# Weight slabs split into high and low parts in halves, in a ring of four half slabs instead of two whole ones

## The chip, the cores and the metric

The kernel runs on one core of a Trainium2 chip. The metric is the device time of one launch in microseconds (us), as the median of several runs. Five engines work side by side and meet only at semaphores: TensorE (PE) does the matrix products, VectorE (DVE) and ScalarE (ACT) the elementwise work, GpSimd (POOL) some more of it, and SyncE (SP) issues the DMAs. Each engine works through its own instructions in the order in which they are written.

## The reference, cut to what matters

Two transformer-like blocks in float32 on a sequence of 512 tokens of width 1024: a convolution block, a squared-ReLU feed-forward layer with a gated per-layer embedding, forgetting attention with a second such layer; then a block with three branches (RG-LRU, block attention, attention to a memory of 256 tokens) and a gated feed-forward layer with a short convolution. Nearly all of the arithmetic is products of activations with weight matrices.

```python
hn = rmsnorm(h, mix_norm[i]);  h = h + conformer_conv(hn, ...)      # layer 0: pw1, 31-tap conv, layernorm, silu, pw2
k, v, c = shared_kv(h, kv_norm, w_kvf, b_f)                         # layer 1
h = h + fox_attention(hn, w_q, w_o, k, v, c)
h = h + square(relu(rmsnorm(h, ffn_norm[i]) @ ffn_w1[i])) @ ffn_w2[i]
h = h + sigmoid(rmsnorm(h, ple_norm[i]) @ w_gate[i]) * (p[i] @ w_proj[i])
# second block
proj = rms_norm(x, mix_norm_gain) @ w_in                            # xa, ga, qm, km, vm, qx, gates
y_a = rg_lru(causal_dwconv(xa, ...)) * gelu(ga); y_b = moba_attention(qm, km, vm); y_c = cross_attention(qx, mem)
x = x + sum_n(gate_n * (y_n @ w_branch[n])) @ w_out
x = x + (gelu(causal_dwconv(h @ w_ffn_gate, ...)) * (h @ w_ffn_up)) @ w_ffn_down
```

## The kernel before, in words

All activations stay in SBUF as (128 partitions = channels, 512 tokens), eight such chunks for a width of 1024. Each float32 product is made of three matmuls on rounded parts: `w_hi*x_hi + w_hi*x_lo + w_lo*x_hi` (`three`, L489 to L492). A rounded part `w_hi` is a copy of the weights by ACT, and `w_lo = w - w_hi` is a subtraction by POOL.

Weights come in 176 slabs of 128x2048 floats. A slab holds two columns of output blocks (8 chunks of 128 rows each), so PE makes two blocks of 24 matmuls from it, each in one of four PSUM banks (`gp`). A slab goes through four hands:

- SP loads it into one of two places of `raw` (`slab`, L281), once POOL has made `w_lo` of the slab two before it (its semaphore `w_lo_done`).
- ACT copies it to `w_hi` (`next_w`, L778 to L786). This is called at chosen places of ACT's program for the slab after the one named, and waits until PE has finished the slab that had the place before (`blk_done`). `w_hi` and `w_lo` have two places each.
- POOL makes `w_lo` (`slab`, L363 to L366), in the order of the slabs, between its other work.
- PE uses it (`slab_ws`, L494; `slab_xs`, L511, where the weights are the moving operand) after `w_lo_done`.

The order is written out by hand for each engine; loops (`Fori`) repeat a body. The places of interest:

- The first convolution (`tap_products` on ACT, L828; `add_taps` on POOL, L414; `conv` on DVE): channels are worked in four pairs of chunks. For a pair DVE multiplies and adds 22 taps, while ACT makes 9 products that POOL adds into `pool_sum` (16 additions for a pair). Within this, the blocks of the next pair are fetched from PSUM (`pair_out`, `T<-gp,rstd`), ACT makes the sigmoids (L826), and slabs of the pair after that are split: at `t == MID_TAP` and at `t == GATE_TAP` on ACT, after `t == 5` and at the end on POOL. Once, in the first pair, DVE also scales the memory (`mem_raw`, eight instructions).
- The start of a feed-forward layer (`ffn_layer`, L931): PE starts on the new slabs while DVE and ACT make `rstd` (`finish_norm`, L803). PSUM banks come free only when `rstd` is there.
- The gates after a feed-forward layer (L958 to L975): for each block DVE does six to seven operations on SBUF tensors and ACT four.
- The RG-LRU (L1087 to L1100, L1595 to L1620): four steps, each a chain of PE, ACT (`lru_hi`, sigmoids, tanh, sqrt) and DVE (seven linked operations `link_l`), beside the blocks of `gqm` and `gkm`.
- The branches (`branch`): DVE multiplies a block with its gate and adds it to `merged`.
- SP waits for POOL's memsets of `wga` and `wgx` (L448, L449) before it loads them, and issues the next slab after them.

## Time and profile before

| | |
|---|---|
| median of 3 runs | 2306.7 us (2306.33 to 2308.54) |
| span of the profiled execution | 2308.7 us (first to last instruction; the page gives no other time of this execution) |
| PE busy | 2153.5 us, 93% |
| DVE, POOL, ACT busy | 1154.3, 939.4, 791.1 us |
| granted TensorE clock, mean | 0.971 of full speed |
| DMA | 196.74 MB, mean 85 GB/s |

The page and the views list instructions by the line of the kernel, the engine, the operation and the tiles (`out<-in`). The busy share alone doesn't say what an engine's work costs: what PE waits for, and when, is in the view of waits and in PE's timeline, where a figure in brackets is the idle time just before an instruction, with what ended it. The line of a helper (L490 to L492, L1146, L1149) stands for all its callers, so the tiles tell which stage a row is of.

### The profile page before, as it was taken

Reading aid. Unit: us, or ns where it says so; the run is one execution under the profiler, and the core shown is the slowest. Engines: PE = TensorE matmul, PEld = TensorE weight load, DVE = VectorE, ACT = ScalarE, POOL = GpSimd, SP = SyncE. Lnnn points to the kernel's source line nnn. Section 1 sums busy time; section 2 is a strip of 40 time slices with the busy share of each in tenths; the row PEclk is TensorE's granted clock in tenths of the full one; section 3 lists DMA queues with packets and bytes.
Section 4 is the critical chain, followed back from the end, with each engine's and each line's share of the span. In section 5 each row is a group of like instructions: output and inputs, shape, how many; then the busy total and the mean of one; then the engine's idle time right before and its main releaser. Section 6 shows DMA issues by size and latency. Waiting matters only on the chain.

```text
span 2308.7 us, 27336 instructions
## 1 busy us (share of the span) xinstructions
PE 2153.5 (93%) x10068; PEld 1764.5 (76%) x10068; DVE 1154.3 (50%) x1624; ACT 791.1 (34%) x1044; POOL 939.4 (41%) x306
## 2 busy tenths in 40 slices
PE   7547999999999999999999998999899999999997
PEld 6445788888878987778888876777777878888885
DVE  5996543233473545462342557328444357445364
ACT  5445422122442146321221344324225243222232
POOL 4785344344343420334444342343253334434332
PEclk9878999999999999999999999999999999999998
DMA  4121222322322211222222321132220222322231
GB/s 178 37 73 55 91 91 93 108 91 91 106 77 93 101 46 36 100 73 98 103 91 93 107 89 58 55 114 73 73 92 1 92 91 91 109 92 91 92 108 55
DMA packets 30717, 196.74 MB, mean 85 GB/s; under 512 B 4384, under 2 KB 4512, under 8 KB 7984
## 3 DMA queue, kind: packets, MB, share of 16 engines
q1 hardware_dynamic: 30640, 195.68, 24.4%
q8 instruction: 52, 0.85, 0.2%
q14 instruction: 25, 0.20, 0.0%
HBM read 193.54 MB, written 2.13 MB: 85 GB/s over the span
## 4 chain that ended last, share of the span: by engine, by line
issue 43%; PE 38%; POOL 13%; DVE 5%; ACT 1%; POOLq 0%; ACTq 0%; DVEq 0%
PE gp L490 11%; PE gp L492 11%; PE gp L491 11%; POOL w_lo L366 11%; PE ms L692 2%; PE gp L644 2%; POOL pool_sum L422 2%; PE ms L629 1%; DVE T L1602 1%; DVE T L1146 1%; DVE U L1601 1%; DVE xc L1149 0%; DVE U L1146 0%; DVE U L1447 0%; DVE merged L1146 0%
## 5 line engine op out<-in xcount | busy, mean ns | idle before, releaser
L366 POOL TENSOR_TENSOR w_lo<-raw,w_hi 128x2048 fp32r<-128x2048 f32 x176 | 813.3, 4621 | 1192.9 <-ACT w_hi L786 1187.4
L490 PE MATMUL gp<-a_hi,w_hi 128*128 128x512 f32 x1440 | 572.4, 397 | 56.9 <-DVE T L1146 27.2
L491 PE MATMUL gp<-a_lo,w_hi 128*128 128x512 f32 x1440 | 566.0, 393 | 0.0
L492 PE MATMUL gp<-a_hi,w_lo 128*128 128x512 f32 x1440 | 565.9, 393 | 0.0
L490 PE MATMUL gp<-b_hi,w_hi 128*128 128x512 f32 (+1 forms) x1216 | 476.0, 391 | 41.3 <-POOL b_lo L434 27.4
L786 ACT ACTIVATE w_hi<-raw 128x2048 fp32r<-128x2048 f32 x175 | 333.5, 1906 | 436.0 <-PE gp L492 431.2
L491 PE MATMUL gp<-b_lo,w_hi 128*128 128x512 f32 (+1 forms) x1216 | 472.6, 389 | 0.0
L492 PE MATMUL gp<-b_hi,w_lo 128*128 128x512 f32 (+1 forms) x1216 | 472.4, 389 | 0.0
L490 PEld LDWEIGHTS gp<-a_hi,w_hi 128*128 128x128 f32 x1440 | 274.2, 190 | 121.8 <-DVE T L1146 28.0
L491 PEld LDWEIGHTS gp<-a_lo,w_hi 128*128 128x128 f32 x1440 | 274.2, 190 | 58.6 <-issue 2.0
L492 PEld LDWEIGHTS gp<-a_hi,w_lo 128*128 128x128 f32 x1440 | 273.7, 190 | 57.8
L490 PEld LDWEIGHTS gp<-b_hi,w_hi 128*128 128x128 f32 x1216 | 230.2, 189 | 94.7 <-POOL b_lo L434 27.8
L1146 DVE TENSOR_TENSOR h<-gp,h 128x512 f32<-128x512 f32 x104 | 71.9, 692 | 411.8 <-PE gp L492 411.8
L492 PEld LDWEIGHTS gp<-b_hi,w_lo 128*128 128x128 f32 x1216 | 230.4, 189 | 46.9
L491 PEld LDWEIGHTS gp<-b_lo,w_hi 128*128 128x128 f32 x1216 | 230.6, 190 | 46.6 <-issue 0.7
L1146 DVE TENSOR_TENSOR T<-gp,rstd 128x512 f32<-128x512 f32 x144 | 98.5, 689 | 301.4 <-PE gp L492 297.7
L1149 DVE SCALAR_TENSOR_TENSOR ms<-u_pad,par,ms 128x512 f32<-128x512 f32 x168 | 111.7, 747 | 0.0
L795 ACT ACTIVATE sqb<-h 128x512 f32<-128x512 f32 x63 | 39.8, 632 | 183.6 <-DVE h L1146 156.3
L1149 DVE SCALAR_TENSOR_TENSOR U<-T 128x512 f32<-128x512 f32 x64 | 100.2, 1566 | 2.2
L422 POOL TENSOR_TENSOR pool_sum<-pool_sum,sqb 128x512 f32<-128x512 f32 x64 | 81.5, 1308 | 26.9 <-ACT sqb L841 26.9
L1042 ACT ACTIVATE T<-T,nmax 128x128 f32<-128x128 f32 (+1 forms) x96 | 53.8, 561 | 64.3 <-DVE U L1447 41.8
L1124 ACT ACTIVATE T<-T,par 128x512 f32<-128x512 f32 x24 | 17.4, 724 | 158.0 <-DVE T L1149 158.0
(255 smaller groups left out, 2100.4 us busy)
## 6 DMA issues: line engine op xcount, KB each, us to landing
raw<-w_hbm SPq DMA_DIRECT2D x176, 1024.0 KB, 4.9
fbias<-negc_scratch SPq DMA_DIRECT2D x16, 256.0 KB, 3.1
h<-x_hbm SPq DMA_DIRECT2D x4, 512.0 KB, 7.1
out_hbm<-h SPq DMA_DIRECT2D x4, 512.0 KB, 2.7
mem_raw<-mem_hbm SPq DMA_DIRECT2D x1, 1024.0 KB, 12.1
p_raw<-p_hbm SPq DMA_DIRECT2D x2, 512.0 KB, 9.1
par<-par_hbm SPq DMA_DIRECT2D x1, 264.5 KB, 5.2
wga<-w_a_hbm SPq DMA_DIRECT2D x2, 64.0 KB, 2.3
```

Of the source, the lines that this page charges most:

```text
L366: g.tensor_tensor(w_lo[:, s], raw[:, s], f32(w_hi[:, s]), ALU.subtract).then_inc(w_lo_done, 1)
L422: g.tensor_tensor(pool_sum[:, s], pool_sum[:, s], sqb[:, s], ALU.add).then_inc(pool_conv, 1)
L490: pe.matmul(o, wh, xh, start=start, stop=False)
L491: pe.matmul(o, wh, xl, start=False, stop=False)
L492: return pe.matmul(o, wl, xh, start=False, stop=stop)
L644: m = pe.matmul(gp[:, s % 2, 0:vw], probT[s % 2][:, kb * P:kb * P + P], v_of(j, s % per, kb), start=(kb == 0), stop=(kb == n_of[s % per] - 1))
L692: pe.matmul(ms[:, s % 2, 0:w], qs[:, hh, qb * P:qb * P + P], k, start=True, stop=False)
L786: act.activation(w_hi[:, s], raw[:, s], ACT.Copy).then_inc(w_hi_done, 1)
L795: act.activation(dst, h[:, c], ACT.Square).then_inc(sq_done, 1)
L1042: return act.activation(prob[:, s % 4, 0:w], prob[:, s % 4, 0:w], ACT.Exp, scale=-1.0, bias=nmax[:, s % 4:s % 4 + 1], accum_out=rsum[:, s ...
L1146: return v.tensor_tensor(o, a, b, op)
L1149: return v.scalar_tensor_tensor(o, a, s, b, op0, op1)
```

## The change

Each slab is still loaded as a whole into `raw`, in two places. But `w_hi` and `w_lo` are now rings of four places of half a slab (128x1024), and a half is one block of 24 matmuls (for `slab_xs`, where all 8 chunks of rows are needed, PE waits for both halves). A half takes every second run of 128 columns of the slab's eight rows (`part`; two runs of 512 of two rows, or of 256 of four, and for `slab_xs` the first or second 1024 elements). ACT's `next_w` copies the half three places ahead (`AHEAD`), once the block before the named one is done. PE's matmuls and their order are the same; the memory's mean comes after the first block of the second slab as before. The calls of `next_w`, and the order of POOL's work, are rewritten.

```diff
+PART = SLAB // 2
+RING = 4
+AHEAD = RING - 1
-        w_hi, w_lo = sb("w_hi", [P, 2, SLAB], F32R), sb("w_lo", [P, 2, SLAB], F32R)
+        w_hi, w_lo = sb("w_hi", [P, RING, PART], F32R), sb("w_lo", [P, RING, PART], F32R)
+        def part(pos, d=0):
+            r = rows_of[pos.const + d]
+            i = pos.slot(4, d)
+            q, n = i % 2, SLAB // r // 2 if r else PART
+            src = raw[:, i // 2].rearrange("p (k c) -> p k c", k=r or 2)
+            src = src[:, q:q + 1] if not r else src[:, :, q * n:q * n + n]
+            return src, lambda ring: ring[:, pos.slot(RING, d)].rearrange("p (k c) -> p k c", k=r or 1)
...
@@ SyncE @@
-                    q.wait_ge(w_lo_done, pos.at(-1))
+                    q.wait_ge(w_lo_done, Pos(2 * pos.const, 2 * pos.step, pos.i).at(-2))
-            slabs(wo["slab"] + 2, gxg["slab"])
+            slabs(wo["slab"] // 2 + 3, br[2]["slab"] // 2 + 3)
             for t, name in ((wga, "w_a"), (wgx, "w_x")):
@@ GpSimd @@
+                src, at = part(pos)
-                g.tensor_tensor(w_lo[:, s], raw[:, s], f32(w_hi[:, s]), ALU.subtract).then_inc(w_lo_done, 1)
+                g.tensor_tensor(at(w_lo), src, f32(at(w_hi)), ALU.subtract).then_inc(w_lo_done, 1)
...
-                    if t == MID_TAP + 2:
-                        slab(Pos(4, 2, i))
+                    if t == MID_TAP + 2 and not extra:
+                        for s in range(2):
+                            slab(Pos(memkv["slab"] + 4 + s))
                 if extra:
-                    slab(Pos(5, 2, i))
+                    for s in range(RING):
+                        slab(Pos(8 + s, RING, i))
...
-            slabs(wo["slab"] + 1, gxg["slab"])
+            slabs(wo["slab"] + AHEAD, br[2]["slab"] + AHEAD)
             g.wait_ge(lo_done, xat["split"] + 4)
             g.memset(wga[:], 0.0).then_inc(wg_zero, 1)
@@ TensorE @@
-                s = sp_.slot(2)
-                cc = 16 // kk
+                s = sp_.slot(RING)
+                cc = 8 // kk
                 pe.wait_ge(w_lo_done, sp_.at(1))
@@ ScalarE @@
             def next_w(sp_, bp):
-                s = sp_.slot(2, 1)
-                act.wait_ge(raw_ready[s], 16 * (sp_.turns(2, 1) + 1))
+                src, at = part(sp_, AHEAD)
+                s = sp_.slot(RING, AHEAD)
+                act.wait_ge(raw_ready[s // 2], 16 * (sp_.turns(RING, AHEAD) + 1))
                 if bp.const > 0:
                     act.wait_ge(blk_done, bp.at())
-                act.activation(w_hi[:, s], raw[:, s], ACT.Copy).then_inc(w_hi_done, 1)
+                act.activation(at(w_hi), src, ACT.Copy).then_inc(w_hi_done, 1)
...
                 pw1_gates(Pos(4, 4, i), lambda n, s, o: colp(i)(n, s, o + 2))
-                next_w(Pos(4, 2, i), Pos(8, 4, i))
+                for s in range(RING):
+                    next_w(Pos(5 + s, 4, i), Pos(5 + s, 4, i))
-            next_w(Pos(1), Pos(2))
+            for s in range(1, 5):
+                next_w(Pos(s), Pos(s))
             pw1_gates(Pos(0), colp(0))
-            next_w(Pos(2), Pos(4))
...
-                    if s == 0:
-                        next_w(sp_, bp)
+                    if k == 0:
                         finish_norm(pw2 if l == 0 else wo)
+                    up_hi(f, Pos(f["slab"] + k), Pos(f["blk"] + k), Pos(fu), H_, k)
...
             for j, (at, s) in enumerate(((gqm, 0), (gqm, 1), (gkm, 0), (gkm, 1))):
-                next_of(at, s)
+                next_of(at, 2 * s)
                 act.activation(T[:, 3], T[:, 2], ACT.Sqrt).then_inc(l_act, 1)
+                next_of(at, 2 * s + 1)
```

How the instructions move at three places. First, GpSimd in the first pair of the first convolution (`pool_sum` are the tap additions), before:

```order
L366 TENSOR_TENSOR w_lo<-raw,w_hi 128x2048
L373 REGISTER_ALU
L373 COMPARE_AND_BRANCH
L422 TENSOR_TENSOR pool_sum<-pool_sum,sqb 128x512 x10
L366 TENSOR_TENSOR w_lo<-raw,w_hi 128x2048
L422 TENSOR_TENSOR pool_sum<-pool_sum,sqb 128x512 x6
L366 TENSOR_TENSOR w_lo<-raw,w_hi 128x2048
```

and in the changed kernel:

```order
L383 TENSOR_TENSOR w_lo<-raw,w_hi 128x1024
L392 REGISTER_ALU
L392 COMPARE_AND_BRANCH
L446 TENSOR_TENSOR pool_sum<-pool_sum,sqb 128x512 x16
L383 TENSOR_TENSOR w_lo<-raw,w_hi 128x1024 x4
```

The slab in the middle of the additions is gone, and four halves stand behind them. ScalarE at the same place (`T` are the sigmoids of the first pair, `pool_sum` and `sqb` the tap products), before:

```order
L805 ACTIVATE rstd<-var 128x512
L820 ACTIVATE mkv<-mem_raw 128x2048
L786 ACTIVATE w_hi<-raw 128x2048
L826 ACT_TABLE_LOAD
L826 ACTIVATE T<-T,par 128x512 x2
L786 ACTIVATE w_hi<-raw 128x2048
L837 ACTIVATE pool_sum<-u_pad,par 128x512 x2
```

and in the changed kernel, where four halves stand ahead of the table load and the sigmoids:

```order
L830 ACTIVATE rstd<-var 128x512
L850 ACTIVATE mkv<-mem_raw 128x2048
L811 ACTIVATE w_hi<-raw 128x1024 x4
L856 ACT_TABLE_LOAD
L856 ACTIVATE T<-T,par 128x512 x2
L867 ACTIVATE pool_sum<-u_pad,par 128x512 x2
```

Second, ScalarE at the start of the second feed-forward layer (`rstd` is its norm, `a_hi<-U` the first parts of the hidden layer), before:

```order
L1048 ACTIVATE p_hi<-p_raw 128x1024
L1050 ACTIVATE sp<-sp 128x4
L786 ACTIVATE w_hi<-raw 128x2048
L805 ACT_TABLE_LOAD
L805 ACTIVATE rstd<-var 128x512
L941 ACTIVATE a_hi<-U 128x512 x2
L786 ACTIVATE w_hi<-raw 128x2048
```

and in the changed kernel:

```order
L1075 ACTIVATE p_hi<-p_raw 128x1024
L1077 ACTIVATE sp<-sp 128x4
L830 ACT_TABLE_LOAD
L830 ACTIVATE rstd<-var 128x512
L811 ACTIVATE w_hi<-raw 128x1024
L952 ACTIVATE a_hi<-U 128x512
L811 ACTIVATE w_hi<-raw 128x1024
```

No split stands between the `sp` instruction and `rstd` any more; the fourth half of the layer comes right behind `rstd`, the fifth one `a_hi` later. Third, GpSimd at the memsets of `wga` and `wgx` (second block), before:

```order
L366 TENSOR_TENSOR w_lo<-raw,w_hi 128x2048
L373 REGISTER_ALU
L373 COMPARE_AND_BRANCH
L448 MEMSET wga 128x512
L449 MEMSET wgx 128x512
L450 MEMSET xap 128x4x3
```

and in the changed kernel, where nine halves of the branch have moved behind the memsets:

```order
L392 COMPARE_AND_BRANCH
L383 TENSOR_TENSOR w_lo<-raw,w_hi 128x1024 x3
L474 MEMSET wga 128x512
L475 MEMSET wgx 128x512
L476 MEMSET xap 128x4x3
L383 TENSOR_TENSOR w_lo<-raw,w_hi 128x1024 x9
```

## Rows read from the trace of the kernel before

**Rows 1.** The page, busy time of PE and share of the span

```profile
PE 2153.5 (93%) x10068; PEld 1764.5 (76%) x10068; DVE 1154.3 (50%) x1624; ACT 791.1 (34%) x1044; POOL 939.4 (41%) x306
```

**Rows 2.** Waits of PE, whole span: releaser, us in total, times, longest

```profile
PE gp L490 <- POOL b_lo L434: 27.4, 1, 27.4
PE gp L490 <- DVE T L1146: 27.2, 2, 15.6
PE gp L490 <- DVE a_lo L1149: 16.7, 6, 12.9
...
PE gp L490 <- POOL w_lo L366: 11.4, 9, 4.5
PE gp L490 <- DVE mkv L1146: 10.4, 1, 10.4
...
PE gp L490 <- DVE a_lo L1146: 4.5, 2, 3.1
PE ms L748 <- ACT T L1094: 3.0, 1, 3.0
PE gp L490 <- DVE b_lo L1149: 2.8, 3, 1.6
PE ms L692 <- DVE T L1146: 2.4, 1, 2.4
```

**Rows 3.** The page's groups: count, busy us, mean ns, idle before and its releaser

```profile
L366 POOL TENSOR_TENSOR w_lo<-raw,w_hi 128x2048 fp32r<-128x2048 f32 x176 | 813.3, 4621 | 1192.9 <-ACT w_hi L786 1187.4
...
L786 ACT ACTIVATE w_hi<-raw 128x2048 fp32r<-128x2048 f32 x175 | 333.5, 1906 | 436.0 <-PE gp L492 431.2
...
L1149 DVE SCALAR_TENSOR_TENSOR ms<-u_pad,par,ms 128x512 f32<-128x512 f32 x168 | 111.7, 747 | 0.0
```

**Rows 4.** GpSimd's timeline, 0 to 330 us: start, length, instruction

```profile
66.47 4.68 POOL L366 TENSOR_TENSOR w_lo<-raw,w_hi 128x2048 fp32r<-128x2048 f32 x1
...
164.51 4.51 POOL L434 TENSOR_TENSOR b_lo<-mem_raw,b_hi 128x2048 fp32r<-128x2048 f32 x1
...
195.99 2.36 POOL L437 TENSOR_TENSOR p_lo<-p_raw,p_hi 128x1024 fp32r<-128x1024 f32 x1
...
255.83 4.60 POOL L366 TENSOR_TENSOR w_lo<-raw,w_hi 128x2048 fp32r<-128x2048 f32 x1 [6.28 <-ACT w_hi L786]
266.71 4.61 POOL L366 TENSOR_TENSOR w_lo<-raw,w_hi 128x2048 fp32r<-128x2048 f32 x1 [6.28 <-ACT w_hi L786]
```

**Rows 5.** ScalarE's timeline in the first convolution

```profile
31.91 1.28 ACT L826 ACT_TABLE_LOAD   x1
...
87.96 1.04 ACT L870 ACTIVATE p_hi<-p_raw 128x1024 fp32r<-128x1024 f32 x1
```

**Rows 6.** DVE's timeline there: eight instructions that scale the memory

```profile
64.52 12.91 DVE L1149 SCALAR_TENSOR_TENSOR mem_raw<-mem_raw,par,U 128x256 f32<-128x256 f32 x8
```

**Rows 7.** PE's timeline, in brackets its idle time before the instruction

```profile
116.50 0.80 PE L490 MATMUL gp<-a_hi,w_hi 128*128 128x512 f32 x1 [11.54 <-DVE T L1146]
...
1394.62 0.50 PE L490 MATMUL gp<-a_hi,w_hi 128*128 128x512 f32 x1 [1.99 <-POOL w_lo L366]
...
1524.41 0.49 PE L490 MATMUL gp<-a_hi,w_hi 128*128 128x512 f32 x1 [1.99 <-POOL w_lo L366]
```

**Rows 8.** DVE's timeline at the start of the second feed-forward layer

```profile
984.97 5.96 DVE L1149 SCALAR_TENSOR_TENSOR sp<-sp 128x4 f32<-128x4 f32 x8
```

**Rows 9.** ScalarE's timeline, at that start and at the second block's branches

```profile
999.67 1.91 ACT L786 ACTIVATE w_hi<-raw 128x2048 fp32r<-128x2048 f32 x1
...
1517.70 1.92 ACT L786 ACTIVATE w_hi<-raw 128x2048 fp32r<-128x2048 f32 x1 [4.76 <-DMA raw<-w_hbm]
```

**Rows 10.** DVE's timeline in the RG-LRU and at the last branch

```profile
1584.03 4.91 DVE L1146 TENSOR_TENSOR U<-U,ga 128x512 f32<-128x512 f32 x1
...
1596.74 4.82 DVE L1602 TENSOR_SCALAR T<-U 128x512 f32<-128x512 f32 x1
...
1842.34 4.88 DVE L1146 TENSOR_TENSOR merged<-merged,T 128x512 f32<-128x512 f32 x1
```

More of the change, by code:

```diff
@@ L92, in build, with phase @@
     led = Ledger()
-    def phase(slabs=0, blks=0, **more):
+    rows_of = []
+    def phase(slabs=0, blks=0, rows=8, **more):
         at = {"slab": led.take("slab", slabs), "blk": led.take("blk", blks)}
+        rows_of.extend(rows if isinstance(rows, list) else [rows] * slabs)
         at.update({k: led.take(k, n) for k, n in more.items()})
@@ L327, in _ @@
             fox_bias(0, 1, True)
-            slabs(gv["slab"] + 2, wo["slab"] + 2)
+            slabs(gv["slab"] // 2 + 2, wo["slab"] // 2 + 3)
             with q.Fori(1, 8) as j:
@@ L340, in _ @@
                                 hbm[name][:, hh].rearrange("j i o -> i j o")).then_inc(wg_ready, 16)
-            slabs(gxg["slab"], NS)
+            slabs(br[2]["slab"] // 2 + 3, NS // 2)
             o_v = out
@@ L404, in copies @@
                     g.wait_ge(mb_ready, 2)
-                slab(Pos(next_slab))
-                g.wait_ge(w_lo_done, next_slab + 1)
+                for s in range(AHEAD):
+                    slab(Pos(next_slab + s))
+                g.wait_ge(w_lo_done, next_slab + AHEAD)
                 with g.Fori(1, n) as j:
@@ L450, in _ @@
             g.memset(xap[:, :, 0:3], 0.0).then_inc(pad_zero, 1)
-            slabs(gxg["slab"], br[1]["slab"])
+            slabs(br[2]["slab"] + AHEAD, br[1]["slab"])
             g.wait_ge(lo_done, lru["split"] + 4)
@@ L597, in ffn_layer @@
                     pe.wait_ge(lo_done, p_split[l]["split"] + 1)
-                slab_ws(Pos(proj[l]["slab"]), Pos(proj[l]["blk"]), (p_hi[l], p_lo[l]), kk=2)
+                for s in range(2):
+                    slab_ws(Pos(proj[l]["slab"] + s), Pos(proj[l]["blk"] + 4 * s), (p_hi[l], p_lo[l]), kk=2)
                 gemm(gate[l], X, ready=f["split"] + 32, hook=lambda: stat(gate[l], f["acc"] + 7))
@@ L723, in c_stats @@
                 m.then_inc(col_stat, 1)
-            gemm(gqx, A, n_slabs=2, ready=fin["split"], hook=c_stats)
+            gemm(gqx, A, n_slabs=4, ready=fin["split"], hook=c_stats)
             for c in range(4):
@@ L812, in _ @@
             act.wait_ge(raw_ready[0], 16)
-            act.activation(w_hi[:, 0], raw[:, 0], ACT.Copy).then_inc(w_hi_done, 1)
+            for s in range(2):
+                src, at = part(Pos(s))
+                act.activation(at(w_hi), src, ACT.Copy).then_inc(w_hi_done, 1)
             act.wait_ge(par_ready, 16)
@@ L816, in _ @@
                 prep(c, A, "mix0", x0, lambda: act.wait_ge(x_ready[c // 2], 16))
+            act.wait_ge(raw_ready[1], 16)
+            src, at = part(Pos(2))
+            act.activation(at(w_hi), src, ACT.Copy).then_inc(w_hi_done, 1)
             next_w(Pos(0), Pos(0))
@@ L915, in up_hi @@
                 next_w(sp_, bp)
-                for c in range(2):
-                    act.wait_ge(full, fu.at(k + c + 1))
-                    act.activation(H_[0][:, k + c], U[:, (k + c) % 2], ACT.Copy).then_inc(hi_done, 1)
+                act.wait_ge(full, fu.at(k + 1))
+                act.activation(H_[0][:, k], U[:, k % 2], ACT.Copy).then_inc(hi_done, 1)
             def last_norm_parts(c):
@@ L978, in _ @@
             act.wait_ge(blk_done, gate[0]["blk"] + 8)
-            for s in range(4):
+            for s in range(8):
                 next_of(gq, s)
@@ L989, in _ @@
                     act.activation(wf_hi[:, :, 0:16], wf[:], ACT.Copy).then_inc(wf_hi_done, 1)
-            for s in range(4):
+            for s in range(8):
                 next_of(gk, s)
@@ L1051, in _ @@
             ffn_layer(1, B, A)
-            for s in range(2):
+            for s in range(4):
                 next_of(gqx, s)
@@ L1070, in branch @@
                     bp = Pos(at["blk"] + 8 * half)
-                    for s in range(3):
-                        next_w(Pos(at["slab"] + 3 * half + s), Pos(at["blk"] + 8 * half + 2 * s))
-                        if s < 2:
-                            for c in range(2 * s, 2 * s + 2):
-                                wait_evac(act, bp, c)
-                                act.activation(T[:, c], T[:, c], ACT.Sigmoid).then_inc(sg_done, 1)
+                    for s in range(6):
+                        next_of(at, 6 * half + s, 8 * half + (s if s < 4 else 2 * s - 4))
+                        if s < 4:
+                            wait_evac(act, bp, s)
+                            act.activation(T[:, s], T[:, s], ACT.Sigmoid).then_inc(sg_done, 1)
             branch(2)
-            for s in range(4):
+            for s in range(8):
                 next_of(gxg, s)
```

258 lines of the change are left out of this document (129 added, 129 removed).

## The prediction

> **What bounds the kernel now.** First the page's busy times: PE is busy for 93% of the span [rows 1], so only PE's idle time, about 7%, can be won, and what any other engine saves counts only where PE waits for it. Then the waits of PE, which say for whom [rows 2]. The splitting is named there directly with 11.4 us in nine waits (`w_lo`), the longest 4.5. The larger ones name other work: the first convolution (`T` 27.2, `POOL b_lo` 27.4, about 13 of the 16.7 of `a_lo L1149`, which is the wait for the first inputs), the RG-LRU (`mkv` 10.4 and `ACT T` 3.0), the gates after the two feed-forward layers (`b_lo L1149` 2.8 and the rest of `a_lo L1149`, about 3.1), and the last branches (`ms L692 <- DVE T` 2.4, `a_lo L1146` longest 3.1). Third, the timelines at these places.
>
> In a steady stretch a slab's `w_lo` starts every 10.88 us (255.83, 266.71) and takes 4.6 [rows 4]; ACT's `w_hi` takes 1.9 [rows 3]. So a slab is split in 6.6 of the 10.88 us of its predecessor's matmuls, and 4.3 us are spare: PE waits for nothing in the feed-forward layers themselves, and halves can win nothing there. One block of 24 matmuls is 5.44 us. The change can only act where ACT comes late to a split, or where POOL's long instruction holds up DVE.
>
> How it holds DVE up: `T<-U`, which runs from 1596.74, takes 4.82 us, `U<-U,ga` 4.91, `merged` 4.88 [rows 10], in each case while a `w_lo` of 4.6 us runs; 0.4 to 0.7 is what such instructions take elsewhere (747 ns is the dearest with 512 elements that stands beside no such wait [rows 3]). The SBUF — State Buffer page of the Trainium skill, section "SBUF: two separate sides", says that DVE instructions with two SBUF inputs, or in a two-port mode, and GpSimd instructions hold a shared port pair in turn, each for its whole length. The trace agrees (4.82 beside a 4.6).
>
> **The change part by part.** I sum on the profiled execution's own scale. The page gives no time for it but the span, 2308.7; this lies 2.0 above the median of 2306.7, and I take those 2.0 off at the end.
>
> *Price of the halves.* 1024 elements cost 2.36 on POOL (`p_lo` [rows 4]) and 1.04 on ACT (`p_hi` [rows 5]), so two halves are 4.72 instead of 4.62, and 2.08 instead of 1.91. Over 176 slabs that is 18 and 31 us of engine time, hidden behind PE's 5.44 per half; where ACT or POOL is on the path it is 0.1 to 0.2 per slab. The source now has runs of 128 elements. The nearest row is `b_lo<-mem_raw`, 2048 elements whose output has runs of 256, at 4.51 [rows 4]: no dearer than the contiguous 4.62. I take no surcharge; the upper bound is a rival below. The GPSIMD Engine Reference of the Trainium skill, section "Elementwise — side-by-side cycle accounting", gives every GpSimd instruction a dispatch cost of its own; the pair of rows puts it at 0.1 us for a slab, so it doesn't change the sum.
>
> *Start of the second feed-forward layer: -4.5.* Before, ACT could split the third slab only after `rstd` and two `a_hi`, at 999.67 [rows 9], and PE waited 4.5 for its `w_lo` (the longest in [rows 2]). `rstd` itself is late, because eight tiny `sp` instructions of DVE, a few tenths each, took 5.96 from 984.97 [rows 8]: a `w_lo` stood beside them. In the changed kernel three halves are ready before `rstd`, and no split stands between `sp` and `rstd`, so the `sp` chain takes some 1.5 and `rstd` comes about 4.5 earlier, near 991.8. Then the fourth half takes 1.04 + 2.36 and is ready at about 995.4; PE wants it after the norm's matmul at about 985 and two more blocks of 5.44, so at 995.7. The wait goes, with 0.3 us to spare. Bounds: 4.5, and 1.1 if the `sp` chain is held up as before (`w_lo` at 999.7 against 996). I take 4.5.
>
> *The gates: -6.0.* Of the `w_lo` waits 2.0 are at 1394.62 [rows 7]; four of 0.4 more are in the two gate stages. Each comes from a `w_hi` that stands in ACT's program behind other work of the same block; with three halves made ahead there are 16.3 us of cover instead of 10.88, so 3.6 go. What is late next is `a_lo`/`b_lo` of DVE, 2.8 + 3.1 here. DVE has about 3.8 us of its own per block in the second gate stage and 3.3 in the first, and was held up for 4.3 in every two: 11.9 of 10.88. With halves it is held up twice for at most 2.4, partly beside `T<-gp`, which reads PSUM. Bounds 0 and 5.9; I take 2.4.
>
> *The memsets of `wga`: -2.0.* At 1517.70 ACT waited 4.76 for a transfer [rows 9], because SP held the slab back until the memsets behind the branch's `w_lo`; PE waited 2.0 for it [rows 7]. Moved ahead by nine halves, the memsets come just after the memory attention, and the four transfers and the slab behind them have 14 us. Nothing late stands behind; bounds 1.5 and 2.0.
>
> *RG-LRU: -4.3.* DVE's chain sets the pace, and PE's waits of 3.0 and 10.4 hang on it [rows 2]; so what the chain saves counts, up to 13.4. Four times a `w_lo` holds the chain up for 4.2 to 4.4 [rows 10]. In the first step the half is issued only at a block's end and DVE waits at most 2.3: 2.8 saved, as much as one step can. In the other three steps the two halves stand back to back, the first begun before DVE asks: DVE waits for what is left of it (1.5), gets in once, then waits for the second (2.3): 3.8 instead of 4.4, 0.5 saved in each. Sum 4.3. Bounds: 0, if POOL's second half comes ahead of DVE and each hold-up stays at 4.4; 9, if DVE's instructions slip between.
>
> *Last branches: -2.9.* `merged` at 1842.34 is held up for 4.2 [rows 10] and delays the merge of all branches, whose wait is the 3.1 of `a_lo L1146`; the same before the block attention, 2.4 [rows 2]. Halves of which DVE meets two hold it up for 1.3 and 1.8: 1.1 and 1.8 saved. The same order of POOL brings the copies for the attention 4 us earlier. Bounds 0 and 5.5.
>
> *Forgetting attention: +0.3.* Three halves instead of a slab stand ahead of POOL's copies; the last ends about when the second pair of copies was due. Bounds 0 and 2.
>
> *The first convolution: +0.8.* Several edits meet here.
> (a) At the start DVE waits for the first half only partly: -0.5. But ACT now has four halves ahead of the table load (1.28 [rows 5]) of the first sigmoids, the last waiting for PE's fourth block: 1.04 + 1.28 - 0.5 = 1.8 later.
> (b) The slab in the middle of the first pair's additions is gone (it was at 66.47 [rows 4]). It stood beside the eight `mem_raw` instructions, which took 12.91 [rows 6] where eight of half of 747 ns need 3; with one or two additions of 1.25 between, about 5.2. DVE is then 6 us ahead (7.7 - 1.7).
> (c) But the passes are now tied in a ring. PE can start on the next pair's blocks only when POOL, behind the additions, has made the first half: sigmoid 0.8, four copies 3.9, products and additions 3.3, first half 2.4, then four blocks 21.8 and about 2.3 for the lower clock that PE has after its idle time (at 116.50 a matmul takes 0.8 instead of 0.4 [rows 7]), and 0.8 for the fetch: 35.5, against 34.2 for DVE's own pass. So DVE loses 1.3 in each of two passes and 1 in the first.
> (d) POOL gets to `b_lo` at 164.7 (164.51 before) and ends the last pair's additions at 195.8 against 196.0: DVE's lead is lost there, since POOL ends last. After that one more copy stands ahead of the silu's table: +1.0.
> Net +0.8. Bounds: -4 (all of DVE's lead kept) and +11 (the lead doesn't come, and (c) is paid in full with POOL's additions behind it).
>
> Sum: -4.5 - 6.0 - 2.0 - 4.3 - 2.9 + 0.3 + 0.8 = -18.6. 2308.7 - 18.6 = 2290.1, less 2.0: **2288**.
>
> **Rivals.**
> A: *the hold-ups stay.* DVE is held up as long by two halves as by one slab, since POOL takes the port back each time; the gates' 2.4, the RG-LRU's 4.3 and the branches' 2.9 don't come: -9.0, 2298. For it: the two halves are issued together in RG-LRU. Against: the eight `mem_raw` took 12.91 beside five POOL instructions, so DVE was let in between each two.
> B: *the convolution's ring is longer than I count*, by 3 us a pass, with the end on POOL: +11 instead of +0.8, 2298. For it: four splits now stand behind all the additions. Against: DVE's lead of 6.
> C: *slower:* the split runs of the source make a half dearer on POOL. Its place is the convolution, where 16 halves and 64 additions are on the ring: there every 0.1 us on a half costs 1.6, and the change turns slower once a half takes 2.36 + 18.6/16 = 3.5 us or more; at 4 us it is +7.6, 2314. Elsewhere 5.44 per half still hides it. Against: `b_lo<-mem_raw` at 4.51.
> D: *no change:* PE's `w_lo` waits go, but the same `rstd`, `xc` and `b_hi` chains come last: only 4 of the 18.6 come, 2303.
>
> **How the numbers follow.** A measurement of this kernel tells 0.2% (4.6 us) from no change. Forecast 0.55 (own range 2283 to 2294), A 0.15, B 0.14, C 0.07, D 0.09. Faster by over 0.2% (below 2302.1): forecast, A, B and a third of D, 0.87; within: 0.06; slower: C, 0.07. The range holds A and B at its upper end, and the RG-LRU's and the gates' upper bounds (5 and 3.5 more) at its lower: 2279 to 2301.
>
> **What would show it.** Right: in the waits of PE `w_lo` falls from 11.4 to under 2; no gap of PE near 1006 and 1524; `sp` takes under 2 us; `mem_raw`'s eight under 7; PE starts on the third pair at about 87 instead of 80.7 and the wait for `POOL b_lo` shrinks to about 20; `mkv` falls to 6 or so; POOL's half 2.3 to 2.4, ACT's 1.04. Wrong: a half on POOL above 2.6; `w_lo` waits of PE in the feed-forward layers; `w_hi` copies that wait for a transfer; the first layernorm's first matmul later than 205 us.

## The result, and the profile after

The changed kernel takes 2290.1 us (median of 4 runs, 2288.6 to 2291.1) against 2306.6: the ratio is 0.9923, with a 95% interval of 0.9909 to 0.9937. Forecast were 2288, with a range of 2279 to 2301. The profiled spans differ by more than the medians do, 19.9 (2308.7 against 2288.8) and not 16.5. A run's time is 1.8 above its span wherever both are on record, so the execution shown of before took about 2310.5, which is 3.8 above its median, and the one of after 2290.6, 0.4 above. What follows place by place adds up to 19.9, and some 3.4 of it are no merit of the change but of which executions were profiled.

The page of the changed kernel, busy time [rows 1] (PE's idle time fell from 155.2 to 140.5; the other 5.2 are busy time, the same matmuls at a higher mean clock):

```profile
PE 2148.3 (94%) x10068; PEld 1763.9 (77%) x10068; DVE 1047.6 (46%) x1624; ACT 816.2 (36%) x1220; POOL 978.5 (43%) x482
```

Its waits of PE, which answer to [rows 2]:

```profile
PE gp L516 <- POOL w_lo L383: 32.2, 2, 21.1
PE gp L516 <- POOL b_lo L460: 22.4, 1, 22.4
PE gp L516 <- DVE a_lo L1176: 18.0, 8, 10.0
...
PE gp L516 <- DVE mkv L1173: 9.1, 1, 9.1
...
PE gp L516 <- DVE a_lo L1173: 4.5, 2, 3.1
PE gp L516 <- DVE b_lo L1176: 3.1, 2, 1.6
...
PE ms L717 <- DVE T L1173: 1.1, 1, 1.1
```

`w_lo` has risen to 32.2, but in two waits, both in the first convolution, where they took the place of `DVE T` (27.2). The nine waits of before, 11.4 in all, are gone. `ACT T` (3.0) is gone too. The waits for DVE in the gates have grown: the longest of `a_lo L1176`, at the first inputs, fell from 12.9 to 10.0, and the total is still 1.3 larger. (That 3.0 is no merit of the change: it is 12.1 and 12.2 in the traces of the first two experiments, whose code up to there is the same, and a few us later PE is only 1.0 ahead.)

The page's groups of the halves, to compare with [rows 3]: 2 x 2431 ns for a slab on POOL instead of 4621, 2 x 1050 on ACT instead of 1906.

```profile
L383 POOL TENSOR_TENSOR w_lo<-raw,w_hi 128x1024 fp32r<-128x1024 f32 x352 | 854.1, 2431 | 1111.2 <-ACT w_hi L811 1097.5
...
L811 ACT ACTIVATE w_hi<-raw 128x1024 fp32r<-128x1024 f32 x349 | 364.5, 1050 | 510.6 <-PE gp L518 510.6
```

PE's timeline at the places of the forecast, in brackets the idle time before (for [rows 7]):

```profile
85.36 0.79 PE L516 MATMUL gp<-a_hi,w_hi 128*128 128x512 f32 x1 [21.12 <-POOL w_lo L383]
...
121.26 0.79 PE L516 MATMUL gp<-a_hi,w_hi 128*128 128x512 f32 x1 [11.07 <-POOL w_lo L383]
...
195.80 3.78 PE L597 MATMUL ms<-u_pad,inv_d 128*128 128x512 f32 x4 [8.78 <-DVE u_pad L1173]
...
1390.30 0.80 PE L516 MATMUL gp<-a_hi,w_hi 128*128 128x512 f32 x1 [3.88 <-DVE a_lo L1176]
1393.50 0.80 PE L516 MATMUL gp<-a_hi,w_hi 128*128 128x512 f32 x1 [1.54 <-DVE a_lo L1176]
...
1622.40 0.58 PE L516 MATMUL gp<-w_hi,a_hi 128*128 128x256 f32 x1 [9.13 <-DVE mkv L1173]
```

DVE's timeline at the same places, start and length (for [rows 6, 8, 10]): `mem_raw` 3.9 instead of 12.9, `sp` 1.5 instead of 6.0, and where DVE still meets a half, 1.1 to 2.1 more than the 0.4 to 0.7 that the instruction takes alone.

```profile
66.27 3.89 DVE L1176 SCALAR_TENSOR_TENSOR mem_raw<-mem_raw,par,U 128x256 f32<-128x256 f32 x8
...
984.33 1.54 DVE L1176 SCALAR_TENSOR_TENSOR sp<-sp 128x4 f32<-128x4 f32 x8
...
1374.52 2.77 DVE L1173 TENSOR_TENSOR h<-h,T 128x512 f32<-128x512 f32 x1
...
1598.05 1.77 DVE L1629 TENSOR_SCALAR T<-U 128x512 f32<-128x512 f32 x1
1599.85 2.76 DVE L1173 TENSOR_TENSOR T<-T,U 128x512 f32<-128x512 f32 x1
...
1823.87 1.82 DVE L1173 TENSOR_TENSOR merged<-merged,T 128x512 f32<-128x512 f32 x1
```

The same matmul can be found in both traces, since PE's order didn't change. How much earlier it starts after than before, place by place, is the account of the whole difference between the two executions:

| place (time before -> after) | ahead by | this place | forecast |
|---|---|---|---|
| after the first convolution (650.08 -> 649.32) | 0.8 | -0.8 | +0.8 |
| after the first gates (692.23 -> 690.25) | 2.0 | -1.2 | gates, together -6.0 |
| forgetting attention (933.66 -> 931.69) | 2.0 | 0 | +0.3 |
| start of the second feed-forward layer (1027.66 -> 1019.42) | 8.2 | -6.3 | -4.5 |
| after the second gates (1459.23 -> 1450.20) | 9.0 | -0.8 | (in the gates) |
| third branch's first slab (1524.41 -> 1513.26) | 11.2 | -2.1 | -2.0 |
| RG-LRU (1644.17 -> 1627.26) | 16.9 | -5.8 | -4.3 |
| block attention (1726.67 -> 1708.45) | 18.2 | -1.3 | -1.8 |
| last branch (1855.00 -> 1835.48) | 19.5 | -1.3 | -1.1 |
| end (span) | 19.9 | -0.4 | |

### The profile page after: what moved, and what is told of

It reads as the page before. It is cut to its first block, busy times and chain, and to the rows that moved or that the text cites. A ratio compares the mean times of both kernels' runs of the same rounds, so it can differ in the third digit from the quotient of the medians.

```text
span 2288.8 us, 28318 instructions
## 1 busy us (share of the span) xinstructions
PE 2148.3 (94%) x10068; PEld 1763.9 (77%) x10068; DVE 1047.6 (46%) x1624; ACT 816.2 (36%) x1220; POOL 978.5 (43%) x482
## 3 DMA queue, kind: packets, MB, share of 16 engines
q1 hardware_dynamic: 30640, 195.68, 24.6%
## 4 chain that ended last, share of the span: by engine, by line
PE 85%; DVE 6%; issue 4%; ACT 2%; POOL 2%; DMA 0%; ACTq 0%; DVEq 0%; POOLq 0%
PE gp L516 26%; PE gp L517 26%; PE gp L518 26%; PE gp L669 2%; PE ms L717 2%; DVE T L1173 1%; PE ms L654 1%; DVE xc L1176 1%; POOL w_lo L383 1%; POOL pool_sum L446 1%; DVE U L1628 1%; DVE U L1474 0%; PE ms L568 0%; PE gp L678 0%; ACT w_hi L811 0%
## 5 line engine op out<-in xcount | busy, mean ns | idle before, releaser
L383 POOL TENSOR_TENSOR w_lo<-raw,w_hi 128x1024 fp32r<-128x1024 f32 x352 | 854.1, 2431 | 1111.2 <-ACT w_hi L811 1097.5
L516 PE MATMUL gp<-a_hi,w_hi 128*128 128x512 f32 x1440 | 572.5, 398 | 57.5 <-POOL w_lo L383 32.2
L811 ACT ACTIVATE w_hi<-raw 128x1024 fp32r<-128x1024 f32 x349 | 364.5, 1050 | 510.6 <-PE gp L518 510.6
L1176 DVE SCALAR_TENSOR_TENSOR ms<-u_pad,par,ms 128x512 f32<-128x512 f32 x168 | 111.6, 744 | 0.0
L1176 DVE SCALAR_TENSOR_TENSOR T<-gpad,par,T 128x512 f32<-128x512 f32 x48 | 83.4, 1737 | 5.2 <-DVE T L1676 0.2
L516 PE MATMUL gp<-w_hi,a_hi 128*128 128x256 f32 x192 | 55.5, 289 | 9.1 <-DVE mkv L1173 9.1
## 6 DMA issues: line engine op xcount, KB each, us to landing
mem_raw<-mem_hbm SPq DMA_DIRECT2D x1, 1024.0 KB, 12.1
```

What stands on the lines that cost most here:

```text
L383: g.tensor_tensor(at(w_lo), src, f32(at(w_hi)), ALU.subtract).then_inc(w_lo_done, 1)
L516: pe.matmul(o, wh, xh, start=start, stop=False)
L811: act.activation(at(w_hi), src, ACT.Copy).then_inc(w_hi_done, 1)
L1176: return v.scalar_tensor_tensor(o, a, s, b, op0, op1)
```

## The experiments

All times are medians; each ratio is against the kernel before, run beside it. The medians of the kernel before lie up to 4.6 us apart from one group of runs to the next (2306.6 to 2311.2), so a difference of a few us between two totals shows little; PE's timeline says what an edit did at its place.

### Did the halves bring the gain, or the new order? (three runs)

**The memsets late.** The edit on the changed kernel (POOL's and SP's loops end earlier or later, nothing else; the loops that follow take up the difference and are left out here):

```diff
-            slabs(wo["slab"] + AHEAD, br[2]["slab"] + AHEAD)      # POOL, ahead of the memsets
+            slabs(wo["slab"] + AHEAD, gxg["slab"])
-            slabs(wo["slab"] // 2 + 3, br[2]["slab"] // 2 + 3)    # SP, ahead of the four loads
+            slabs(wo["slab"] // 2 + 3, gxg["slab"] // 2)
```

> The changed kernel, with only the memsets of wga and wgx and SP's four loads put back to where they stood before (ahead of the first half of gxg). Theory 'the order did it': the slab behind them lands as late as in the kernel before, ACT waits again some 4.8 us for it and PE again about 2.0 us for w_lo; total +2.0, so about 2292. Rival 'the halves did it': a half needs 1.04 + 2.4 us after landing instead of 1.9 + 4.6, which is 3.0 less than before and more than PE's old wait of 2.0, so ACT waits but PE doesn't; total +0, about 2290.

Measured: 2289.8, ratio 0.9909 (0.9891 to 0.9927). ACT waits for the late slab, 8.39 and not 4.76 as before, yet PE has no wait there:

```profile
1506.03 1.06 ACT L811 ACTIVATE w_hi<-raw 128x1024 fp32r<-128x1024 f32 x1 [8.39 <-DMA raw<-w_hbm]
```

So the halves alone remove this wait; moving the memsets was not needed. The forecast's term had the right size and the wrong reason.

**A half ahead of the norm.** `next_w(...)` stands ahead of `finish_norm(...)` again in the changed kernel's `ffn_layer`.

> The changed kernel, with the first half of each feed-forward layer's copies back ahead of the norm's square root (the order of the kernel before, with halves). Theory 'halves': one half of 2.4 stands beside the eight sp instructions, which take about 3.9 instead of 1.5, and rstd comes 2.3 later, at about 993; but the fourth half no longer waits for rstd, so PE doesn't wait for it: total +0 to +0.5. Rival 'order' (the gain at this place is the norm that comes first): PE's wait for w_lo comes back with at least 2 us and a stretch at the lower clock behind it, +2 to +5.

Measured: 2289.6, ratio 0.9909 (0.9891 to 0.9927). DVE's `sp` take 3.7, the norm comes later, and PE waits for neither:

```profile
983.09 3.70 DVE L1178 SCALAR_TENSOR_TENSOR sp<-sp 128x4 f32<-128x4 f32 x8
```

**The norm first, with whole slabs.** The kernel before, with the same two lines swapped:

```diff
-                        next_w(sp_, bp)
                         finish_norm(pw2 if l == 0 else wo)
+                        next_w(sp_, bp)
```

> The kernel BEFORE, with one edit: in the feed-forward layers the norm's square root comes ahead of the first copy of a whole slab. Theory: sp takes 1.5 instead of 6.0, rstd comes near 991, but the whole slab behind it needs 1.9 + 4.6 and is ready at about 997.8, where PE wants it at 996: PE's wait of 4.5 shrinks to about 2, total -2.5 against before, up to -5 if no stretch at the lower clock follows the shorter wait. Rival 'halves are needed': no gain, within 1 us. Rival 'order alone': all of it, wait gone, -4.5 to -7.

Measured: 2319.3, ratio 1.0040 (1.0026 to 1.0054), slower. All three theories missed. PE waits longer (7.56 instead of 4.55), and in the first feed-forward layer too, where it hadn't waited at all. PE's timeline:

```profile
291.12 0.80 PE L490 MATMUL gp<-a_hi,w_hi 128*128 128x512 f32 x1 [5.76 <-POOL w_lo L366]
...
1007.24 0.79 PE L490 MATMUL gp<-b_hi,w_hi 128*128 128x512 f32 x1 [7.56 <-POOL w_lo L366]
```

This execution runs 8.9 us later here than the one of before, because of the wait at 291 and the lower clock behind it. On the time scale of before, `rstd` came 4.4 earlier, as expected, and the slab behind it was ready at 998.3, nearly as expected (997.8). But it is one slab earlier in PE's order than the one that PE waited for before, and PE wanted it at 990.8, some 5 us before the estimate of 996. Whole slabs give only one slab ahead, 10.88 us of matmuls; three halves give 16.3, and with them the same order costs nothing. The halves carry this place too; the new order does not. (A ring of three whole slabs wasn't run, so how much is the length of the lead and how much the size of the pieces stays open.)

### What held mem_raw up

The kernel before; in the first pair the slab stands behind POOL's additions (`if t == MID_TAP + 2 and mid:`, and behind the loop `if not mid: slab(Pos(4, 2, i))`, with `add_taps(0, mid=False)`).

> The kernel BEFORE, with one edit: in the first pair of the convolution the slab in the middle of POOL's additions is split behind them. Theory: it was what held up mem_raw: the eight instructions take 4 to 5 instead of 12.9, DVE reaches the end of the first pair some 8 us earlier; but two whole slabs then stand behind the additions and PE starts on the third pair only after the first of them, so that the ring is at least as long as with halves: the last POOL addition ends within 2 us of before (196), total -1 to +2. Rival: the additions themselves hold mem_raw up (they share the port too): mem_raw stays above 9.

Measured: 2304.5, ratio 0.9974 (0.9962 to 0.9986). DVE's timeline, and PE's at the first layernorm matmul:

```profile
64.49 8.66 DVE L1151 SCALAR_TENSOR_TENSOR mem_raw<-mem_raw,par,U 128x256 f32<-128x256 f32 x8
```

```profile
194.93 3.78 PE L575 MATMUL ms<-u_pad,inv_d 128*128 128x512 f32 x4 [9.46 <-DVE u_pad L1148]
```

Between the theories: 4.3 of the 12.9 were the slab, which was moved. The other 4.8 beyond 3.9 belong to the additions, which in this kernel still run beside `mem_raw` (61.27 to 72.1). In the changed kernel POOL has done the additions of this stretch at 67.1, just as `mem_raw` begins, hence 3.9 there and not the forecast's 5.2. The total was expected between -1 and +2 and fell by more: by 2.1 against the first median of before, by 6.7 against the one run beside it. Of the 6.0 between the two traces 2.0 are there at the first layernorm matmul, and 2.7 came by the clock at the last branch, where the code is the same (shown in the part on the prediction).

### The gates: phase or length (two runs)

**The copy right behind the square.**

```diff
                             square(c - 1, g)
+                            if c < 8:
+                                next_of(g, c)
                             last_norm_parts(c - 1)
```

> The changed kernel, with one edit: in the gates after both feed-forward layers ACT copies the half one or two instructions earlier in each block, right behind the square, ahead of b_hi (first gates) or of U and a_hi (second gates). Theory 'phase': in the changed kernel every half meets DVE's h<-h,T just as it starts and holds it up for 2.1, so that DVE's block is 5.87 instead of PE's 5.44; 1.3 earlier, part of the half lies beside T<-gp, which isn't held up, and the hold-up falls to about 1.5: DVE's block 5.44 or less, PE's two waits for a_lo (3.9 and 1.5) fall to about 2 in sum: -2.5 to -4, about 2287. Rival 'length': a half costs DVE 2.1 wherever it stands: no change, 2290.

Measured: 2292.6 (2288.1 to 2294.2), ratio 0.9922 (0.9904 to 0.9940). No gain, where -2.5 to -4 was expected. Still, the hold-up falls even to 0.5, and DVE waits 1.1 for PE in each block of the second gates; but the last half meets the last block, which has no `T<-gp` ahead of it, and PE waits 4.4:

```profile
1377.78 1.13 DVE L1177 TENSOR_TENSOR T<-T,big 128x512 f32<-128x512 f32 x1
...
1386.83 2.85 DVE L1177 TENSOR_TENSOR T<-T,big 128x512 f32<-128x512 f32 x1
```

```profile
1391.73 0.80 PE L516 MATMUL gp<-a_hi,w_hi 128*128 128x512 f32 x1 [4.40 <-DVE a_lo L1180]
```

**And the last copy behind the stage** (`if c < 7`, and `next_of(g, 7)` behind the loop).

> As the kernel with the gates' copies right behind the square, and the last of each stage's eight copies is put behind the stage's last block. Theory: with the copies behind the square DVE keeps up with PE (5.44 a block, 1.1 us idle), but the last half lay beside T<-T,big of the last block and held it up for 2.2, which PE's wait of 4.4 contained; without it PE waits about 2.2 at the end of the second gates and about 1.5 at the end of the first (3.5): the block after the gates starts 3 to 4 us earlier than in the changed kernel; total -3, about 2287, give or take 1.5 for what the clock does behind the later waits. Rival: the chain of a_lo sets the wait whatever stands beside it: PE's wait stays above 4.

Measured: 2284.0, ratio 0.9891 (0.9876 to 0.9906). PE's largest wait there is 2.24:

```profile
1383.21 0.50 PE L516 MATMUL gp<-a_hi,w_hi 128*128 128x512 f32 x1 [0.37 <-DVE a_lo L1181]
...
1386.41 0.50 PE L516 MATMUL gp<-a_hi,w_hi 128*128 128x512 f32 x1 [2.24 <-DVE a_lo L1181]
...
1388.28 0.79 PE L516 MATMUL gp<-a_hi,w_hi 128*128 128x512 f32 x1 [0.80 <-DVE a_lo L1181]
```

The block that waited 3.88 in the changed kernel starts 3.5 us earlier (1383.21 against 1390.30, less the 3.6 that this execution was ahead before); at the end of the stage 2.3 of that are left, and the first gates gave nothing. So the edit is worth 2 to 3 us at its place, as expected, and the total shows 6.1. Of the 3.6, 2.8 are no merit of the edit: they arose at 934, where this execution had the higher clock earlier.

### The RG-LRU: shorter instructions or better places (three runs)

**Quarters.** POOL's half in two instructions of 512 elements, in the whole program.

> The changed kernel, with POOL's w_lo of each half made by two instructions of 512 elements a partition. Theory 'in turn': DVE is held by each of POOL's instructions in turn, so the sum of the hold-ups in a block stays about 2 (one of 2.1 becomes 0.9 and 1.2), and the quarters cost 0.1 more per half: the gates' DVE block stays 5.8 to 6.0, the RG-LRU's step 15.6 to 16.2, total 0 to +2. Rival 'DVE slips between': each hold-up is at most 1.2 and only the first counts: DVE's block falls below 5.44, the RG-LRU's step to about 14.5, total -4 to -8.

Measured: 2289.9, ratio 0.9918 (0.9901 to 0.9934). DVE's timeline in the second gates:

```profile
1362.60 1.71 DVE L1175 TENSOR_TENSOR h<-h,T 128x512 f32<-128x512 f32 x1
1364.23 1.78 DVE L1175 TENSOR_TENSOR acc_sq<-acc_sq,sqb 128x512 f32<-128x512 f32 x1
```

One hold-up of 2.1 has become two of 1.0 and 1.1, one behind the other. The RG-LRU's step is 15.5 instead of 15.8, the gates' block 5.6 on average. Where DVE has instructions queued up, it and POOL take turns, and DVE pays for nearly POOL's whole time, whatever the pieces. It isn't so everywhere: DVE's busy time falls by 28.4 over the program (1047.6 to 1019.2), and PE waits 7.0 instead of 9.1 at `mkv`, 2.9 ahead there. A third of that is lost again to the lower clock by 1870, and the total doesn't show the rest.

**The copy ahead of the square root** (`next_of(at, 2 * s + 1)` two lines earlier).

> The changed kernel, with one edit: in each RG-LRU step the second copy of ACT comes ahead of the square root instead of behind it. Theory: POOL's half then starts 1.0 to 1.5 earlier and lies beside DVE's reciprocal (3.35), which has one SBUF input and isn't held up; of the two hold-ups of 1.3 and 2.1 in a step one goes or both shrink, to 2.2 in sum; the step falls from 15.8 to about 14.6, PE's wait at mkv from 9.1 to about 5.5; total -3.6. Rival: the square root comes 1.04 later and DVE waits for it: no gain.

Measured: 2290.4, ratio 0.9915 (0.9898 to 0.9931). At the place itself it is as expected: a step takes 14.5, PE's wait at `mkv` is 5.0, and PE is 3.7 ahead there. But the total doesn't move. The 3.7 shrink to 1.3 behind the wait at 1762 and to 0.2 behind that at 1833, each time by a longer stretch at the lower clock (mean granted clock 0.72 instead of 0.84 over 10 us, and 0.55 instead of 0.76 over 7 us).

**POOL paced by DVE's chain**, on top of it:

```diff
-            slabs(br[2]["slab"] + AHEAD, br[1]["slab"])
+            slabs(br[2]["slab"] + AHEAD, gqm["slab"] + AHEAD + 2)
+            for j in range(4):
+                g.wait_ge(l_y, j + 1)                  # DVE has made U<-U,ga of this step
+                slabs(gqm["slab"] + AHEAD + 2 * j + 2, gqm["slab"] + AHEAD + 2 * j + 4)
+            slabs(gqm["slab"] + AHEAD + 10, br[1]["slab"])
```

> As the kernel with the copy ahead of the square root, and POOL waits, before the other half of each RG-LRU step, until DVE has made that step's U<-U,ga (behind which DVE reads PSUM and then waits for ACT). Theory: both halves of a step then lie where DVE doesn't ask for the port, the hold-ups in a step fall from 3.4 to at most 0.7, the step from 15.8 to about 13, where PE sets the pace; PE's wait at mkv of 9.1 all but goes; total -8 to -10, about 2281. Rival: the paced half comes too late for PE, which waits for w_lo in each step instead: total -3 or less.

Measured: 2276.5 (2276.3 to 2277.4), ratio 0.9857 (0.9841 to 0.9874). The wait at `mkv` is gone, a step is 12.64 and follows PE. DVE's and POOL's timelines of one step:

```profile
1583.56 0.69 DVE L1177 TENSOR_TENSOR U<-U,ga 128x512 f32<-128x512 f32 x1
1584.17 1.28 DVE L1180 SCALAR_TENSOR_TENSOR qm<-gp,rstd 128x512 f32<-128x512 f32 x2
1585.37 1.92 DVE L1177 TENSOR_TENSOR b_lo<-U,b_hi 128x512 fp32r<-128x512 f32 x1
1588.20 0.43 DVE L1631 TENSOR_SCALAR U<-T 128x512 f32<-128x512 f32 x1 [0.92 <-ACT T L1128]
1588.66 3.35 DVE L1632 RECIPROCAL U<-U 128x512 f32<-128x512 f32 x1
```

```profile
1584.33 2.41 POOL L383 TENSOR_TENSOR w_lo<-raw,w_hi 128x1024 fp32r<-128x1024 f32 x1 [4.52 <-DVE U L1177]
1590.06 2.41 POOL L383 TENSOR_TENSOR w_lo<-raw,w_hi 128x1024 fp32r<-128x1024 f32 x1 [3.31 <-ACT w_hi L815]
```

The two edits together carry this run. The first half lies beside `qm<-gp` (which reads PSUM and takes its usual time), holds `b_lo` up by 1.2, and there DVE has 2.1 to spare before `U<-T`; the second lies beside the reciprocal. Of the 13.6 gained, 9.9 are at `mkv` and another 2.3 follow because PE, without the pause, keeps the higher clock behind it.

### The convolution's ring, and the best version (three runs)

**Halves in the middle of the additions**, in the second and third pair (two of four, on ACT at `MID_TAP` and on POOL after `t == MID_TAP + 2`).

> The changed kernel, with one edit: in the second and third pair of the first convolution two of the four halves are copied and split in the middle of the additions (the first pair keeps all four behind them). Theory 'ring': PE then has two blocks' halves when DVE fetches the last pair, so it starts 11 us earlier in each pass and the passes fall from 35.7 and 34.9 to DVE's own 34.2; behind the third pair only two halves stand ahead of b_lo instead of four (4.7 us less), and POOL's last addition, at 194.9, comes at about 188; the first layernorm matmul at about 189 instead of 195.8; total -6 to -7, about 2283.5. Rival 'POOL': POOL has no idle time to give, the halves in the middle only delay the additions: the last addition within 2 us of 194.9.

Measured: 2285.2, ratio 0.9895 (0.9880 to 0.9911). The first layernorm matmul comes 4.8 earlier than the 195.80 of the changed kernel's trace; seven other executions in which this part is the same or has only shorter pieces have it between 194.13 and 196.16, so the edit gave 3 to 5:

```profile
162.71 0.58 PE L519 MATMUL gp<-b_hi,w_hi 128*128 128x256 f32 x1 [27.16 <-POOL b_lo L463]
190.99 3.78 PE L600 MATMUL ms<-u_pad,inv_d 128*128 128x512 f32 x4 [8.78 <-DVE u_pad L1179]
```

The third pass is DVE's 34.1, as expected; the second isn't (36.3), since PE still starts its blocks at 85.39, behind the first pair's four halves, and DVE waits 0.8 for PE and 0.6 for ACT. Hence less than the 6 to 7 expected.

**Three edits together** (paced, in the middle, gates): 

> The changed kernel with three edits together: the paced halves of the RG-LRU, the halves in the middle of the convolution's additions, and the gates' copies behind the square with the last one late. Theory: the three places are far apart and add up: -13.6 measured for the first, -6.5 and -3 expected of the others: 2267, between 2264 and 2271. Rival: part of it is given back at a later wait (that of the feed-forward layers or of the attention): above 2273.

Measured: 2262.9 (2262.3 to 2270.8), ratio 0.9815 (0.9797 to 0.9834). That is 1.1 below the expected range. By the medians 13.6 + 4.9 + 6.1 would be 24.6, and it is 27.2; by the ratios, which compare with runs side by side, the three are 15.2, 6.5 and 7.4, in sum 29.1, and it is 24.9. So they add up within what these totals can show.

**And the pause of the first pair** (two halves and the memory's `b_lo` behind `g.wait_ge(mscaled, 8)` ahead of its last two additions; ACT's copies ahead of the sigmoids):

> The version with three edits, and a fourth: in the first pair of the convolution two halves of the next pair and b_lo of the memory are split in POOL's pause of 13 us before its last two additions, once mem_raw is scaled (70.2), instead of behind the additions of the first and the third pair. Theory: DVE isn't held up there (its sums and fetches read PSUM); PE starts on the third pair at about 75 instead of 85.3, the second pass falls from 36.3 to DVE's 34.2, and 4.5 us of b_lo leave the stretch in which POOL ends last, so that DVE itself ends last: first layernorm matmul 4 us earlier than in the version with three edits (189.9), total about -4.4 against its 2262.9: 2258.5. Rival: what POOL gives up is given back at once, by DVE (held up at u_pad) or by ACT, whose sigmoids come later: less than 2 us.

Measured: 2265.3 (2259.7 to 2266.3), ratio 0.9811 (0.9798 to 0.9825): not to be told from the version with three edits. PE's timeline shows its mechanism at work, 2.8 ahead of the 189.89 of that version:

```profile
73.47 0.80 PE L530 MATMUL gp<-a_hi,w_hi 128*128 128x512 f32 x1 [9.21 <-DVE T L1198]
...
187.13 3.43 PE L611 MATMUL ms<-u_pad,inv_d 128*128 128x512 f32 x4 [19.25 <-DVE u_pad L1198]
```

`u_pad` was held up by 1.3, as its rival had it, so 2.8 there instead of 4. The five times fall in two groups (2259.7 to 2259.9 at a mean granted clock of 0.981; 2265.3 to 2266.3 at 0.977 or 0.978), those of the version with three edits as well (2262.3 to 2262.9 at 0.981; 2270.2 and 2270.8 at 0.976). Where in the program the lower clock falls is open, since both traces are of the higher group.

## Why the prediction was right, and where its terms were not

The time was right to 2.1 us, but terms of both signs were off, and that they cancel is luck: the gates gave 4.0 less than forecast, and the convolution, the start of the second feed-forward layer and the RG-LRU 4.9 more, largely through the clock. The correction of 2.0 at the end compared a span with a time. It did no harm, since the sum is in effect taken off the median, 2306.7 - 18.6; but the sum is 18.6 against a measured 16.5, and the 19.9 of the traces hold the 3.4 named above. How such a difference comes about is seen behind the last branch's wait of 3.07, which is the same in the kernel before and in its variant with the slab moved in the convolution. The code there is the same too, but the granted clock (third number from the end) isn't:

```profile
1852.00:1860.00 8.00, 7.27 (x20) 5.78 (x21) 4.80 (x8) 5.31 (x8) 2.61 (x1) 0.59 0.00 0
```

```profile
1848.00:1856.00 8.00, 7.30 (x32) 6.10 (x33) 5.46 (x9) 6.06 (x10) 2.63 (x1) 1.00 0.00 0
```

20 matmuls in 8 us against 32: 2.7 us without any edit there.

- **Price of the halves:** as taken, 2.43 and 1.05 in the mean, some of it hold-ups by DVE. Rival C is out, and so are B (the convolution's passes are as counted, below) and D (only 4 us come).
- **Start of the second feed-forward layer:** the wait of 4.55 went, as forecast. Behind a wait PE ran at the lower of its two clocks (1.2 of 2.4 GHz), and that went too. The windows of the two traces just behind the place, with the granted clock as the third number from the end:

```profile
1006.00:1012.00 6.00, 5.79 (x14) 4.53 (x15) 1.30 (x2) 2.43 (x2) 2.91 (x2) 0.50 0.51 175
```

```profile
1004.00:1010.00 6.00, 6.00 (x28) 4.97 (x27) 4.67 (x4) 1.97 (x3) 4.14 (x2) 1.00 0.25 72
```

  14 matmuls in 6 us against 28: worth 2.9 us in these two executions, which the forecast left out everywhere but in the convolution. Part of it can be chance: between 1000 and 1020 the variant with the slab moved is 1.1 quicker than the kernel before, with the same wait. Elsewhere it goes the other way: at 934, behind a wait of 1.41 in both, the changed kernel lost 1.2. The forecast's reason (the `sp` chain) is true as a description, but the two runs on the norm's place show that it isn't what the gain hangs on: with halves and the norm late PE waits for nothing, with whole slabs and the norm first it waits longer.
- **The gates, -6.0 forecast, -2.0 measured: the step that failed.** The 3.6 of `w_lo` waits went. But of "held up twice for at most 2.4, partly beside `T<-gp`" the second part was wrong: ACT's copy follows from DVE's own `h`, so each half meets the next `h<-h,T` at its start, 2.1 in every block once the stage runs evenly, and twice 2.1 is as much as the 4.3 of one slab. In the second gates DVE's block is 5.87, more than PE's 5.44, and over both stages PE's waits for DVE grew from 5.9 to 8.7 where they were to fall by 2.4. The runs with the copy moved show that the phase sets the hold-up (2.1 or 0.5). It isn't the whole of the miss: at the better phase, with the last copy late, PE still waits 5.4 for DVE in the two stages, which with the `w_lo` waits gone is 4.1 less than before; 6.0 were forecast.
- **The memsets:** -2.1, forecast -2.0, by another cause (the shorter path from landing to `w_lo`).
- **RG-LRU, -4.3 forecast, -5.8 measured.** PE's two waits there, 13.4 in all, fell by 4.3, just the forecast sum; the other 1.5 are clock behind the wait that is gone. Inside the sum the terms were off both ways. In a later step DVE is let in between the halves, as forecast, and the hold-ups are 1.3 and 2.1 (mean step 15.8 against 16.7), 1.0 saved instead of 0.5; that leaves some 1.4 for the first step instead of 2.8. The sign "`mkv` falls to 6" missed (9.1), because the 3.0 of `ACT T` went instead.
- **Last branches, -2.9 forecast, -2.6 measured,** of which the forecast's cause gave only 1.3, at the block attention. At the last branch the wait is 3.06 as before (3.07): the hold-up of `merged` at 1842.34 had been made up when the last block ended, since its `T<-gp` (1849.79) stood 0.1 behind PE, as in the changed kernel. What came there is clock, and the comparison above shows that it is the clock of the execution and not of the change. A hold-up three blocks ahead of an end was counted as if it stood at the end.
- **Forgetting attention:** 0.
- **First convolution, +0.8 forecast, -0.8 measured,** which is no more than equal code differs by there (PE's first layernorm matmul at 196.89 and 197.89 in two executions of the old one). The ring is there: passes of 35.7 and 34.9 (forecast 35.5), PE's starts at 85.4 and 121.3, `b_lo` late. `mem_raw` gave 9.0 instead of 7.7, and the last addition ended at 195.0, 0.8 before the forecast. The sign "`w_lo` falls to under 2" could not come true beside this ring: PE's two starts behind the additions are `w_lo` waits of 32.2.

Rival A (the hold-ups stay) was true in the gates and only in part in the RG-LRU (3.4 instead of 4.4 a step); it is a question of phase at each place, not of one rule. Its reason, "POOL takes the port back each time", is what the quarters show. The Trainium skill's SBUF — State Buffer page, section "SBUF: two separate sides", has whoever starts first keep the shared ports for its whole instruction. The traces agree (2.77 beside a half), and add that with both queues full the two alternate (1.0 and 1.1 with quarters), so that in the gates and the RG-LRU shorter pieces alone hardly shorten DVE's loss.

## What to carry to other kernels

Finer pieces in a ring pay first by the cover that they give (three halves ahead are 16.3 us of matmuls, one slab 10.88) and by the shorter way from landing to use. Shorter hold-ups came only in part: 1.0 a step in the RG-LRU, nothing in the gates. Where a GpSimd instruction holds VectorE up, place it beside VectorE's PSUM reads (`qm<-gp`, 1.28 for two as usual), its reciprocal (3.35 as usual) or its own waits, with a semaphore if need be: in the RG-LRU that was worth 13.6 us, almost as much as the whole change. One input alone doesn't make an instruction safe: `T<-U` (`TENSOR_SCALAR`), 0.43 alone, took 4.82 beside a slab and 1.77 beside a half. And ask at each stage what releases the copy: if it is the held-up engine itself, the collision repeats in every block.
